# Moving the transposes of the gathered rows behind the down product in the expert loop of a streaming encoder step

## What is computed

```python
    def run_block(args):
        xb_i, e = args
        hid = jax.nn.silu(xb_i @ w_gate[e]) * (xb_i @ w_up[e])
        return hid @ w_down[e]

    yb = lax.map(run_block, (xb, blk_e))
    y = jnp.zeros((T + 1, D), f32).at[buf_tok].add(yb.reshape(P, D).astype(f32) * buf_w[:, None])
```

## Time and profile before

| | us |
|---|---|
| median of three runs | 1568.57 |
| the profiled execution: its own time | 1571.97 |
| the profiled execution: span from first to last instruction | 1570.2 |
| TensorE busy | 1413.9 (90%) |
| VectorE busy | 964.3 (61%) |
| ScalarE busy | 831.0 (53%) |
| GpSimd busy | 298.4 (19%) |

### The profile page before, as it was taken

How to read it: one execution, slowest core, us unless ns; L and a number is a source line. 1 busy time by engine, 2 the same in 40 slices (tenths; PEclk the granted TensorE clock), 3 DMA queues, 4 the chain that set the end, 5 groups by cost and what they waited for, 6 DMA issues and landing times. The chain is left out here.

```text
span 1570.2 us, 22689 instructions
## 1 busy us (share of the span) xinstructions
PE 1413.9 (90%) x8018; PEld 1203.7 (77%) x8018; DVE 964.3 (61%) x1157; ACT 831.0 (53%) x1096; POOL 298.4 (19%) x332
## 2 busy tenths in 40 slices
PE   5999999999999999999996059999999999999970
PEld 4999999999999999999996037676666666666650
DVE  5544444654444465544443258998888888888853
ACT  5535433643543364444322147877777777777732
POOL 1002112100211210011200412212232222223213
PEclk9999999999999999999998569999999999999995
DMA  7235336332533643343332379999999999999946
GB/s 284 95 99 186 111 132 220 136 121 95 181 118 127 216 141 114 102 148 121 121 114 81 121 285 381 366 367 377 377 377 377 376 373 372 373 377 378 377 150 250
DMA packets 72903, 357.97 MB, mean 228 GB/s; under 512 B 10961, under 2 KB 11234, under 8 KB 47730
## 3 DMA queue, kind: packets, MB, share of 16 engines
q1 hardware_dynamic: 59122, 317.60, 54.3%
q0 software_dynamic: 9824, 25.28, 6.9%
q10 hardware_dynamic: 3888, 14.16, 2.3%
HBM read 329.71 MB, written 27.75 MB: 228 GB/s over the span
## 5 line engine op out<-in xcount | busy, mean ns | idle before, releaser
L1343 DVE TENSOR_TENSOR wlo<-est,whi 128x2048 fp32r<-128x2048 f32 x193 | 441.1, 2291 | 119.5 <-ACT whi L1339 91.7
L1339 ACT ACTIVATE whi<-est 128x2048 fp32r<-128x2048 f32 x193 | 369.3, 1916 | 157.3 <-DMA est<-wexp 124.8
L819 DVE TENSOR_TENSOR w<-stage,w 128x1024 fp32r<-128x1024 f32 x171 | 222.8, 1324 | 83.5 <-ACT w L560 81.8
L560 ACT ACTIVATE w<-stage 128x1024 fp32r<-128x1024 f32 x171 | 175.5, 1055 | 109.1 <-PE ps L1051 102.7
L1701 PE MATMUL ps<-whi,xT 128*96 128x512 f32 x512 | 205.9, 402 | 26.7 <-DVE xT L1651 26.2
L1703 PE MATMUL ps<-whi,xT 128*96 128x512 f32 x512 | 203.9, 398 | 0.0
L1702 PE MATMUL ps<-wlo,xT 128*96 128x512 f32 x512 | 202.9, 396 | 0.0
L1049 PE MATMUL ps<-w,hT 128*128 128x384 f32 x576 | 199.9, 347 | 1.7 <-DVE w L819 1.7
L1051 PE MATMUL ps<-w,hT 128*128 128x384 f32 x576 | 193.2, 335 | 0.0
L1050 PE MATMUL ps<-w,hT 128*128 128x384 f32 x576 | 192.9, 335 | 0.0
L1049 PE MATMUL ps<-hT,w 128*128 128x384 f32 x408 | 139.0, 341 | 2.5 <-DVE hT L813 2.5
(11 more groups left out here) (220 smaller groups left out, 2396.3 us busy)
## 6 DMA issues: line engine op xcount, KB each, us to landing
est<-wexp SPq DMA_DIRECT2D x193, 1024.0 KB, 13.9
stage<-wmix SPq DMA_DIRECT2D x171, 512.0 KB, 3.6
xn<-x_all SPq DMA_DIRECT2D x9, 512.0 KB, 4.5
xTs<-xT_all SPq DMA_DIRECT2D x6, 768.0 KB, 8.1
XR<-x_all SPq DMA_DIRECT2D x9, 512.0 KB, 6.6
x_scratch<-XR ACTq DMA_DIRECT2D x9, 512.0 KB, 2.8
h_scratch<-h2n ACTq DMA_DIRECT2D x9, 512.0 KB, 3.7
cx<-x_scratch SPq DMA_DIRECT2D x9, 512.0 KB, 8.9
```

The source lines that it names most:

```text
L560: act.activation(whl[w % 2][0][:, q * PIECE:(q + 1) * PIECE], stage[r % STAGE][:], ACT.Copy)\
L819: vec.tensor_tensor(whl[w % 2][1][o], stage[r % STAGE][:], whl[w % 2][0][o].bitcast(F32), ALU.subtract)\
L1339: act.activation(whi[q][:], est[q][:], ACT.Copy).then_inc(e_hi[q], 1)
L1343: vec.tensor_tensor(wlo[q][:], est[q][:], whi[q][:].bitcast(F32), ALU.subtract).then_inc(e_lo[q], 1)
```

## The change

In the loop over blocks, TensorE does the down product of block b first and the transposes of the gathered rows of block b+2 after it. The steps ahead of the loop and behind it stay, as do the orders of all other engines.

```diff
@@ -1762,8 +1762,8 @@
             hid_transposes(1)
             with pe.Fori(1, second_last) as b:
                 gate_up(b + 1, False)
+                down(b)
                 x_transposes(b + 2)
-                down(b)
                 hid_transposes(b + 1)
             gate_up(last, False)
             down(second_last)
```

## The result

The changed kernel takes 1653.04 us (median of four runs, 1651.95 to 1655.04) beside 1568.67 for the kernel before: a ratio of 1.054, 95% interval 1.052 to 1.056. The direction was right; the forecast of 1587.0 and the range up to 1600 were not. Of 84 us, 18 had been forecast.

The account below looks back on a forecast made before the run. Loads bound most passes, TensorE the rest; the new chain was to set the pass at 16.78 + 0.83 + 1.70 = 19.31 us. Over 29 passes: 560.0 less 541.6, 18.4 us more; 1568.57 + 18.4 = 1587.0 us, range 1577 to 1600.

Parts of the forecast that it names:

- The hand-over: Last row transpose through ScalarE's copy and VectorE's subtraction to `gate_up`: 1.70 us exposed each pass, making it 19.31 us.
- Loads: Loop loads: 7.0 MB a pass takes 18.7 us at 374 GB/s, under 19.31, so old waits vanish.
- The gather: On GpSimd: issued no later despite moved transposes; the 1.9 us of TensorE waits for gathered rows should vanish.
- The queues it moves past: Work queued on VectorE, ScalarE, the loads and GpSimd: VectorE has 1.4 us left a pass, so delays cost nothing.
- Slower by more: Rival: VectorE's 1.4 us do not suffice, late loads or list pieces add 0.5 us a pass: 1601.5 us; chance 0.09.
- The clock falls: Rival: TensorE's gap without ordinary matmuls lowers its clock, 2.9 us a pass, 85 us more, about 1672; chance 0.02.

Follow-up runs that it names:

- Two runs that cut the ring: Changed kernel with pair weights in a tile of their own, 1583.54 us; changed kernel with `yS` scaled by a constant column, 1586.81 us.
- one that shortens the scatter in it: Changed kernel with VectorE's weight subtraction behind `hidT` held until GpSimd has issued the scatter: 1586.4 us.
- the semaphore: GpSimd's signal that the scatter is issued, awaited by VectorE before its weight subtraction: changed kernel 1586.4 us, kernel before 1568.73 us.
- without the wait for the list piece: Changed kernel with `yS` scaled by a constant column, so that only the scatter waits for the list piece: 1586.81 us.
- the two more subtractions: Changed kernel with two more PSUM subtractions on VectorE ahead of that of `hidT`: 1675.96 us.

## Why the prediction was wrong

*The hand-over.* Right, to 0.03 us a pass: 19.28 against 19.31. Two runs that cut the ring and one that shortens the scatter in it come to 1583.5, 1586.8 and 1586.4 us, where the forecast was 1587.0. The clock's gap of 2.53 us at ordinary passes was harmless, as the prediction held from the gap of 2.28.

*Loads.* Right: no part of the wait came on top of another for a load, and the old waits went. The rate fell further than to 362 GB/s, since the passes were longer; in the three runs just named it was 363 to 365. (One load is served in 2.8 us, not 2.7; nothing hangs on it.)

*The gather.* Right: no transpose waited for gathered rows. That the gather would be issued no later was not: GpSimd waited for the moved transposes 41 us in ten stops, without making a scatter late.

*The queues it moves past.* This step failed. I had put the order on VectorE in time and found 1.4 us to spare, which was enough for an ordinary pass (VectorE idles 2.1 to 2.4 us ahead of `x_lo` there, at 1101.91, 1121.19 and 1166.93). I had put GpSimd in one sentence: behind the gather stands the scatter, "whose rows come later still". I costed that at nothing without following the scatter to its end. The ring is scatter, landing, list piece, `yS`, next scatter. In the trace of before, with a scatter of 3.2 us, the list piece released ScalarE's `yS` at 1125.00. VectorE's, at 1125.74, had not waited for it; had it started at 1125.00 too, the next scatter could have begun 0.74 + 0.84 us later, at 1126.58, which is 18.2 us after 1108.42. In a pass of 19.31 that leaves 1.1 us, less than the 1.4 on VectorE. A scatter of 7.6 us is 4.4 longer, and the ring is then the longest chain by some 3 us, as an estimate; measured, it took 24.56 us (1110.08 to 1134.64), for landing took longer as well. Nor did I ask what makes a scatter take 3.2 us in some blocks and 1.5 in others. The answer is VectorE, whose work after `yS` I had just laid out: by my own times it runs from 9.2 to 24.9 without a gap. That is the very thing that blocks the scatter.

*The rivals.* "Slower by more" named the list pieces that hold `y_out` back, but with 9% and 0.5 us a pass; it was 66 us over 29 passes, 2.3 each, of which 45 are stops and 21 the clock. I had taken the size from the old waits, and the new one has its own size, three weight subtractions. "The clock falls" had the right price (up to 2.9 us; measured 2.0 to 2.7 in nine passes) and the wrong gap: it took the 2.53 us of an ordinary pass, and a late one has 6.2. I treated the two as alternatives, and the first brings on the second.

What stays open is when GpSimd gets its way between two instructions of VectorE that follow without a gap: after the third weight subtraction in the changed kernel, after the first with the semaphore, mostly after the second without the wait for the list piece, and only after the fourth with the two more subtractions. And what the clock cost by itself was read from durations, not shown by a run that removes it.

## What to carry to other kernels

When an order moves, follow each ring that passes through a DMA and comes back (here scatter, list piece, `yS`) and compare its length with the new pass; a ring with 1.1 us to spare is the next bound once one of its links grows by more, whatever the busy shares say. An operation that takes two different times in a trace has a second party, and it should be named before the change is priced, since the change may lengthen exactly that. And filling an engine's gaps is not free for its neighbour: VectorE's waits for loads were what let GpSimd in.

## What the runs showed of the hardware

A scatter issued by GpSimd takes 1.5 us by itself. It is held back while VectorE runs subtractions with two operands in SBUF, and then ended 1.36 to 1.39 us after one of them ended, in both kernels. Held by one such instruction it took 3.2 to 3.6 us there and in the runs with the semaphore, by three 7.6, and by four, with `hid` between them, 11.3. In the trace of before, the twelve scatters of 3.2 us or more each began 0.19 to 0.46 us into a weight subtraction; of the 20 others none began more than 0.04 us into one. The Trainium skill, "SBUF — State Buffer", Who interferes with whom, says that VectorE and GpSimd share a port, and that an instruction of VectorE with two SBUF inputs contends with a GpSimd instruction that reads SBUF; these rows agree. Its section on the two sides of SBUF describes a DMA of GpSimd's starved by VectorE only for VectorE's 2-port modes; the rows show it for these subtractions (3.2 us in place of 1.5).

After 6.2 us in which TensorE had done only transposes, the granted clock of the next `gate_up` was 0.82 on average (2.2 us lost); gaps of 2.5 us with transposes in them, 20 times in the loop of the changed kernel, left `gate_up` at its 11.2 us and, in the stretches read, the clock at 1.00.
